# Shared expert's four up blocks moved from the combination into the routing stage and behind the third expert

## What is computed

```python
def swiglu(x, w1, w3, w2):
    return (jax.nn.silu(x @ w1) * (x @ w3)) @ w2

def moe_ffn(xs, router_w, router_bias, exp_w1, exp_w3, exp_w2, sh_w1, sh_w3, sh_w2):
    scores = jax.nn.sigmoid((xs @ router_w).astype(jnp.float32))
    ...                                   # idx, w: the 6 experts of a token and their weights
    yg = lax.map(expert_block, (xg, blk_e)).reshape(P, D) * slot_w[:, None]
    routed = jax.ops.segment_sum(yg, slot_tok, num_segments=T + 1)[:T]
    return routed + swiglu(xs, sh_w1, sh_w3, sh_w2)
```

## Time and profile before

| | us |
|---|---|
| median of 3 runs | 2116.54 (2116.13 to 2123.39) |
| the profiled execution's own time | 2121.22 |
| its span in the trace | 2119.4 |
| TensorE matmul busy | 1847.9 (87%) |
| TensorE weight load busy | 983.2 (46%) |
| VectorE busy | 864.2 (41%) |
| ScalarE busy | 458.9 (22%) |
| GpSimd busy | 389.3 (18%) |
| moved by DMA | 625.11 MB, mean 295 GB/s |

### The profile page before, as it was taken

One profiled execution on the slowest core, in us unless ns is written; L12 is line 12 of the kernel. 1 busy time (PEld: TensorE's weight loads), 2 busy tenths in 40 slices (PEclk: granted clock), 3 DMA queues, 4 the chain that ended last, 5 costly groups with the idle time before them and its releaser, 6 DMA issues.

```text
span 2119.4 us, 30756 instructions
## 1 busy us (share of the span) xinstructions
PE 1847.9 (87%) x9520; PEld 983.2 (46%) x9521; DVE 864.2 (41%) x1525; ACT 458.9 (22%) x823; POOL 389.3 (18%) x577
## 2 busy tenths in 40 slices
PE   5999999886998889887999998877888899988996
PEld 3455555434544444444444443344444444544543
DVE  1556767566322222222116499575222212222226
ACT  4144444221111011111011554330111111111112
POOL 0010000011111111111105388012111111111113
PEclk9999999997999999999999999898999999999998
DMA  9488011357999999999988102257999999999955
GB/s 402 182 335 339 1 40 48 151 218 269 397 410 402 398 394 393 404 399 394 373 357 307 76 1 119 86 243 280 391 405 403 399 395 406 390 406 392 395 185 209
DMA packets 95681, 625.11 MB, mean 295 GB/s; under 512 B 16128, under 2 KB 16256, under 8 KB 57472
## 3 DMA queue, kind: packets, MB, share of 16 engines
q1 hardware_dynamic: 44640, 499.70, 58.7%
q0 software_dynamic: 26112, 79.72, 10.4%
q10 hardware_dynamic: 24864, 44.84, 5.8%
HBM read 563.38 MB, written 76.28 MB: 302 GB/s over the span
## 4 chain that ended last, share of the span: by engine, by line
PE 56%; DMA 26%; DVE 8%; POOL 5%; issue 3%; ACT 2%; SPq 0%; POOLq 0%; ACTq 0%; DVEq 0%
DMA ring<-in 23%; PE PS L1171 10%; PE PS L1165 9%; PE PS L1178 5%; PE PS L1192 4%; PE PS L1203 4%; PE PS L1392 3%; POOL work L649 3%; PE PS L1129 3%; PE PS L1082 3%; PE PS L1053 2%; PE PS L1120 2%; PE PS L1015 2%; PE PS L1092 2%; POOL work L617 2%
## 5 line engine op out<-in xcount | busy, mean ns | idle before, releaser
L1171 PE MATMUL PS<-ring,work 128*64 128x256 f32 x3360 | 420.1, 406 | 112.9 <-DMA ring<-in 91.9
L1171 PEld LDWEIGHTS PS<-ring,work 128*64 128x64 f32 x3360 | 260.7, 146 | 248.4 <-DMA ring<-in 97.8
L1581 DVE TENSOR_TENSOR work<-work,PS 64x256 f32<-64x256 f32 x105 | 44.4, 423 | 524.9 <-ACT work L716 523.0
L1178 PE MATMUL PS<-ring,work 128*64 128x512 f32 x840 | 203.3, 605 | 1.3 <-DVE work L1593 1.2
L1165 PE MATMUL PS<-ring,work 128*128 128x512 f32 x400 | 184.1, 615 | 22.4 <-DMA ring<-in 16.1
L569 POOL COPY col_i<-idx 128x1 int32 (+1 forms) x128 | 23.4, 182 | 799.9 <-PE PS L1203 792.4
L1587 DVE COPY work<-PS 128x1024 f32<-128x1024 f32 x128 | 156.8, 1225 | 16.7 <-PE PS L1203 12.8
L575 POOL DMA_INDIRECT work<-h_rows,col_i x128 | 125.1, 978 | 166.0 <-issue 166.0
L1203 PE MATMUL PS<-cst,work 128*128 128x128 f32 x1040 | 142.4, 281 | 14.0 <-DMA work<-h_rows,col_i 14.0
L716 ACT ACTIVATE work<-PS 64x256 f32<-64x256 f32 x105 | 39.5, 376 | 517.9 <-PE PS L1171 515.6
L1203 PEld LDWEIGHTS PS<-cst,work 128*128 128x128 f32 x1040 | 115.0, 142 | 67.1 <-issue 52.4
(11 more groups left out here) (264 smaller groups left out, 2200.7 us busy)
## 6 DMA issues: line engine op xcount, KB each, us to landing
ring<-in SPq DMA_DIRECT2D x156, 2048.0 KB, 8.6
ring<-in SPq DMA_DIRECT2D x132, 1024.0 KB, 10.8
y_rows<-sq POOLq DMA_DIRECT2D x2, 14336.0 KB, 59.5
y_rows<-work ACTq DMA_DIRECT2D x210, 128.0 KB
ring<-in SPq DMA_DIRECT2D x3, 4096.0 KB, 15.4
y_rows<-work ACTq DMA_DIRECT2D x46, 256.0 KB
ring<-in SPq DMA_DIRECT2D x2, 3072.0 KB, 17.2
work<-in SPq DMA_DIRECT2D x2, 2048.0 KB, 17.0
```

The source lines that it names most:

```text
L1171: last = mm(bank(6)[64 * q:64 * q + 64, 0:F], lhs(c)[:, 0:64], w13(s)[:, q, c, :], start=(c == 0), stop=(c == DC - 1), tile_position=(0, 6 ...
L1178: last = mm(bank(4)[64 * q:64 * q + 64, :], actT[par][:, kk, 0:64], w2(s)[:, kk, q * 512:(q + 1) * 512], start=(kk == 0), stop=(kk == 1), ...
```

## The change

The four blocks and what feeds them move. Block (0,0) goes behind the transposes of the scores, a chunk each time ScalarE has written one of `hM` (in ScalarE's order, 6, 0, 7, 1, 2, 3, 4, 5). Of block (0,1) one chunk goes behind the first count matmul and one behind the next two, and six behind the last two; seven chunks of (1,0) follow, and the eighth goes behind the transposes of the first expert's rows. Block (1,1) goes behind unit 2 and waits for VectorE's table of result rows. They use PSUM banks 6, 5, 4 and 3. The silus and products move along. The up half of the shared weights is loaded into `work[:, 0:4096]`, where `acc` lies: in layer 0 with the router's weights once attention's matmuls are done, ahead of the last two units of the modulation's weights, and in layer 1 behind the convolution's layer norm, ahead of the last such unit. Since `acc` is taken, the rows are staged in the two gather buffers `xg` and the two result buffers `yb`, and ScalarE waits for their stores before it writes the first result there. The two clears of `xg` on GpSimd go; `prod_a` shares a tile with `prod_b`; the products of the shared expert get a tile of their own, `shared_sb`; and `dynamic_dma_scratch_size=8192` replaces the default of 16384. Two waits are added ahead of the shared down. Its core:

```diff
-        prod_a = work[:, TT * D:TT * D + NK * E].rearrange("p (k t e) -> p k t e", k=K, t=TT)
+        prod_a = prod_b = hT[:, DC * T + DC * E:DC * KEYS].rearrange("p (k t e) -> p k t e", k=K, t=TT)
+        staged = xg + yb
+        sh_up = work[:, 0:UP]
+        SHARED_BANK = (6, 5, 4, 3)
...
-                sp.wait_ge(m["up_ps"], E - 3)
-                sp.dma_start(slot_ap(SHARED)[:, 0:UP], sh_w[i][:, 0:UP]).then_inc(sh_in, 16)
...
-            for u in range(WO_UNITS, LATE):
+            for u in range(WO_UNITS, LATE - 2):
                 load_unit(u)
             sp.wait_ge(o_ps, NPAIR)
             load_router(0)
+            load_shared(0)
+            for u in range(LATE - 2, LATE):
+                load_unit(u)
...
-            for u in range(LATE, UNITS):
+            for u in range(LATE, UNITS - 1):
                 load_unit(u)
+            sp.wait_ge(nrm_out, 8 * J_LN + DC)
+            load_shared(1)
+            load_unit(UNITS - 1)
...
-                for n in range(2):
-                    nc.gpsimd.memset(xg[n], 0.0).then_inc(cleared, 1)
...
-                    A(acc[:, t, :], bank(1 if t % 2 == 0 else 4, 2), ACT.Copy).then_inc(hrow_sb, 1)
+                    A(staged[t], bank(1 if t % 2 == 0 else 4, 2), ACT.Copy).then_inc(hrow_sb, 1)
...
+                a.wait_ge(hd_out, 64 * (i + 1))
                 either(0, lambda big: store(0, 0, 0, big))
...
+                def shared_up(blk, a, chunks, wait=None):
+                    for c in chunks:
+                        if wait:
+                            wait(c)
+                        last = mm(bank(SHARED_BANK[2 * blk + a]), sh_w13[:, a, c, blk * 128:blk * 128 + 128], hM[:, c, :],
+                                  start=(c == SHARED_ORDER[blk, a][0]), stop=(c == SHARED_ORDER[blk, a][-1]))
+                        if c == SHARED_ORDER[blk, a][-1]:
+                            last.then_inc(sh_ps, 1)
...
-                pe.wait_ge(nrm_out, 8 * (J_FFN0, J_FFN1)[i] + DC)
+                pe.wait_ge(sh_in, 16 + 32 * i)
+                shared_up(0, 0, APPLY_ORDER, lambda c: pe.wait_ge(nrm_out, 8 * (J_FFN0, J_FFN1)[i] + APPLY_ORDER.index(c) + 1))
...
+                pe.wait_ge(hrow_sb, TT + i * TT)
+                shared_up(0, 1, range(0, 1))
...
+                shared_up(0, 1, range(1, 2))
...
+                shared_up(0, 1, range(2, DC))
+                shared_up(1, 0, range(0, DC - 1))
                 turn_rows(0, 16, 0)
+                shared_up(1, 0, range(DC - 1, DC))
...
                 unit(2, slot_of(2), slot_of(1), 32, 32, 0)
+                pe.wait_ge(rows_rdy, i + 1)
+                shared_up(1, 1, range(DC))
...
-                pe.wait_ge(sh_in, 32 * (i + 1))
-                shared_up(0, 0)
...
-                shared_up(0, 1)
-                pe.wait_ge(sh_gate, 1 + 2 * i)
-                shared_up(1, 0)
-                pe.wait_ge(sh_act, 1 + 2 * i)
-                shared_up(1, 1)
+                pe.wait_ge(sh_in, 32 * (i + 1))
                 pe.wait_ge(sh_act, 2 + 2 * i)
...
                 extra_rows()
+                shared_product(0)
                 rows_out(0, 0, 0)
...
                 act_out(2, 1, 0)
+                shared_product(1)
...
-                    if n == 10:
-                        shared_product(1)
...
-    nc = _bacc.Bacc("TRN2", target_bir_lowering=False, num_devices=1)
+    nc = _bacc.Bacc("TRN2", target_bir_lowering=False, num_devices=1, dynamic_dma_scratch_size=8192)
```

More of the change, by code:

```diff
@@ L202, in build @@
         select_to_cmpa = work[:, at_select:o[0]]
-        shared = [work[:, at_select - TT * E + n * T:at_select - TT * E + (n + 1) * T] for n in range(2)]
+        shared_sb = sb("shared_sb", [128, 2 * T])
+        shared = [shared_sb[:, n * T:(n + 1) * T] for n in range(2)]
         assert o[0] <= 12800
@@ L429, in load_router, with load_shared @@
                 sp.dma_start(bias_sb[:, :], router_bias[i].partition_broadcast(128)).then_inc(rw_in, 16)
+            def load_shared(i):
+                sp.dma_start(sh_up, sh_w[i][:, 0:UP]).then_inc(sh_in, 16)
             def load_moe(i):
@@ L749, in store, with shared_silu @@
                          .then_inc(y_out[par], 16)
+                def shared_silu(blk):
+                    a.wait_ge(sh_ps, 2 * blk + 1 + 5 * i)
+                    A(shared[blk], bank(SHARED_BANK[2 * blk]), ACT.Silu).then_inc(sh_gate, 1)
+                shared_silu(0)
                 a.wait_ge(big_rdy, i + 1)
+                shared_silu(1)
                 either(0, lambda big: silu(0, 0, 0, big))
                 either(1, lambda big: silu(1, 0, 1, big))
+                a.wait_ge(hd_out, 64 * (i + 1))
                 either(0, lambda big: store(0, 0, 0, big))
@@ L764, in moe @@
                 a.sem_inc(m["t_yev"], 1)
[L766 to L770, removed]
                 a.wait_ge(unit_rdy, i + 1)
@@ L1230, in rows_of @@
                     last.then_inc(hrow_ps, 1)
+                def shared_up(blk, a, chunks, wait=None):
[6 more added lines that the diff above has]
+                            last.then_inc(sh_ps, 1)
+                SHARED_ORDER = {(b, a): APPLY_ORDER if (b, a) == (0, 0) else range(DC) for b in range(2) for a in range(2)}
                 pe.wait_ge(scoreT_rdy, i + 1)
@@ L1290, in moe @@
                 unit(0, slot_of(0), None, 32, 16, 0)
+                pe.wait_ge(sh_gate, 2 + 3 * i)
                 unit(1, slot_of(1), slot_of(0), 32, 32, 1)
@@ L1307, in moe @@
                 either(E - 1, lambda big: down(E - 1, 1, slot_of(E - 1), big))
-                def shared_up(blk, a):
-                    for c in range(DC):
-                        last = mm(bank(3 * a), w13(SHARED)[:, a, c, blk * 128:blk * 128 + 128], hM[:, c, :], start=(c == 0), stop=(c == DC - 1))
-                    last.then_inc(sh_ps, 1)
-                pe.wait_ge(sh_in, 32 * (i + 1))
-                shared_up(0, 0)
                 many = nc.tensor.value_load(unit_i[0:1, XMAX:XMAX + 1], min_val=0, max_val=XMAX)
@@ L1711, in weights, with shared_product @@
                                                 wsum.unsqueeze(1).to_broadcast([128, K, TT]), ALU.mult, ALU.mult))
+                def shared_product(blk):
+                    dve.wait_ge(sh_ps, 2 * blk + 2 + 5 * i)
+                    dve.wait_ge(sh_gate, blk + 1 + 3 * i)
+                    V.tensor_tensor(shared[blk], shared[blk], bank(SHARED_BANK[2 * blk + 1]), ALU.mult).then_inc(sh_act, 1)
                 dve.wait_ge(count_ps, 3 + 3 * i)
```

18 lines of the change are left out of this document (9 added, 9 removed).

## The result

The changed kernel takes 2125.75 us (median of 20 runs, 2121.58 to 2133.73) and the kernel before, over its own 20 runs, 2120.71 (2113.03 to 2125.58). The ratio is 1.0028 with a 95% interval of 1.0019 to 1.0037: slower by 5.9 us (4.0 to 7.8), and so within the half per cent called no change. Forecast were 2125.0 us and +8.5 us. The forecast difference lies a little above that interval. That the time itself came out 0.75 us from the forecast is partly luck: the kernel before came out 4.2 us above the three runs known at the time.

What follows compares the result with a forecast made beforehand. Each expert loop was taken to end when its weights have come through DMA (busy share 1.01); 8.6 + 9.0 - 7.4 - 1.7 = +8.5 us on the median 2116.54 gave 2125.0 us, range 2109 to 2134.

Steps and rivals of the forecast that it cites:

- term 1: Start of each expert loop: fifteen chunks ahead of the first expert delay its up and the first refill request, +8.6 us.
- term 3: End of each loop: without block (0,0) the extra unit's up starts earlier, then waits for its weights, -7.4 us.
- Term 2: Behind the third expert: block (1,1) delays refill requests, paid less what the DMA queue had in store, +9.0 us.
- the 2.2 + 1.8 + 1.0 of the prediction: Behind the third expert: queue's store in layers 0 and 1, and layer 1's idle time filled ahead of unit 3's up.
- Term 4: The combination: blocks leave TensorE, shortening VectorE's wait in layer 0, and the second product leaves VectorE's chain, -1.7 us.
- (a): Expert loops: the loop absorbs both delays at its start, about 2107.5 us or 2104; chance 0.16.
- (b): Routing stage: TensorE's clock falls within block (0,0), delaying the row transposes, some 5 us a layer, 2135 us; chance 0.14.

Runs made afterwards that it cites:

- the one with slots exchanged: Changed kernel with the ring slots of the extra unit and of the shared down weights exchanged; ratio 0.9995 to the kernel before.
- the first two kernels: The kernel before, and that kernel with only the scratch for GpSimd's descriptors halved (8192 for 16384), ratio 0.999.

## Why the prediction was right, and where it was off

**The direction and the whole were right:** a small loss, +5.9 us against a forecast of +8.5, from two delays at the loops' start, less a gain at their end. By the table, the loops end 6.6 us a layer later than before (627.3, the mean of the changed kernel and the one with slots exchanged, against 620.6, the mean of the first two kernels), 13.2 together; the extra unit gives 2.7 a layer back (the ten layers of the changed kernel, of (1,1) twice and of the three kernels with blocks in mid-loop and slots not exchanged have a mean of 19.3, against 22.05), 5.4 together; what is left to 5.9 is -1.9. That the sum came within 2.6 us of the measured difference is in part luck: term 1 was too high and the gain of term 3 too large, and the two errors go against each other.

**Term 2, block (1,1), +9.0:** right in place, mechanism and, nearly, in size. Moved away alone it gave 10.8 us by the ratio and 2 x 4.9 by the loops' ends; doubled, it cost its full length. The queue's store of 2.2 and 1.8 us was read from the earlier trace rows, and the changed kernel's DMA view shows it used up. TensorE's timelines show where it was used. Take the end of a unit's up, counted from the end of its layer's first up, against the mean of the first two kernels (which differ by up to 3.2 us in this). In layer 0 of the changed kernel unit 3 is 6.9 us late, unit 8 3.6, unit 30 4.2 and the last 3.9; with (1,1) twice the same units are 13.7, 10.3, 9.3 and 9.4 us late. Some 3.3 us are made good once, within five units, and the rest stays. In layer 1 of the changed kernel it is 6.3, 4.7, 4.9 and 7.1. With three blocks in mid-loop, unit 27 of layer 0, behind the second of them, is 4.0 us late and unit 30 only 0.2.

**Term 1, the fifteen chunks, +8.6: mis-sized.** The first up ended 1.1 and 4.8 us later against its layer's scores, 5.9 together; averaged over the kernels that keep the chunks up to there (changed, slots exchanged, doubled, (1,1) moved) and against the mean of the first two, 1.1 and 3.6, so 4.7. The step that failed is the start of the sum. It put the first count matmul where it was; that came 1.4 and 1.7 us earlier. Counted from there, the first up did end 2.6 and 6.4 us later, as forecast. Most of the 1.4 and 1.7 is that the two clears on GpSimd, taken at nothing, had slowed VectorE's one-hot matrices by a us: put back, they bring the count matmul to +24.4, of +24.6 and +24.9 before. The 2.5 us that the sum adds behind the count matmuls, and the 3.0 of its high end, were the author's estimate for chunks at the lower clock, set between what two other groups had lost after idle time, 2.0 us of 5.68 and 3.0 of 17.00; no run shows either for the chunks. In their place the changed kernel's trace showed 2.3 us in layer 0, with a granted clock of 0.50 from 490 to 495 us and 0.85 in the next 5, and in layer 1 2.07 + 2.07 + 12.58 - 13.1 = 3.6, with 0.50 from 1430 to 1435 us and 0.65 in the next 5. The first up did keep full clock behind the chunks: 3.67 us in both layers, at a granted clock of 1.00. What reached the first up goes on to the loop's end where the block doesn't follow: with the block in mid-loop the loops end 1.8 us a layer later than before (622.4 against 620.6). In the whole time the chunks' price stays open between 5.7 us (fourteen left out) and nothing (fifteen gone, two blocks in mid-loop). By the first-up column the two delays bring 4.7 + 14.0 us to a pair of loops that ended 13.2 later: 5.5 us were swallowed once, near the 2.2 + 1.8 + 1.0 of the prediction, and the lateness of the units puts that behind the block, as the prediction did.

**Term 3, the loops' end, -7.4:** the right wait, named in advance, at 5.4 on average; in the changed kernel's own trace it is 3.7 in layer 0 and 0.4 in layer 1. The extra's weights came 10.2 us after their issue in layer 0 and 13.5 in layer 1, against 11.2 and 10.4 before, and the wait and the slower up after it were as forecast. (By the earlier trace rows the up was to start 5.4 and 5.6 us earlier, not 5.3 and 5.5, which would have made the term -7.6.) That the weights were what was late next is shown by the exchange of slots, which took 7.0 us off.

**Term 4, the combination, -1.7:** about -1.9 by what is left over, which is a remainder and no measurement. In the two traces the stretch from the end of the extra unit's down to the end of VectorE's residual went from 52.6 to 50.0 us in layer 0 and from 54.1 to 51.0 in layer 1, and what follows the last residual from 15.6 to 17.0; but the kernel before with half the scratch has 52.0 and 51.9 for that stretch, so the size isn't settled. VectorE's wait for the last transposes came to 0.89 us in both layers, where 0.8 had been forecast for layer 0 and no change for layer 1. TensorE's last 16 transposes did run at a lower clock in both layers, 3.78 and 3.79 us at a granted clock of 0.50; in layer 1 of the kernel before they took 2.05 us at 1.00.

**The rivals.** (a) falls: delays ahead of requests weren't absorbed, as the doubled block shows. Its premise holds elsewhere, though: in the middle of the loop three blocks of 7 us a layer left no gap in the part of the stream that was read, and their lateness was gone a few units later. At the loop's start it did not hold. (b) falls: the granted clock was 1.00 from 470 to 478 us, through block (0,0), and the row transposes took 1.91 us and started 1.0 us later than before.

## What to carry to other kernels

In a kernel like this one, work of an idle engine is cheap inside a stretch that waits for transfers only where the transfers' queue has more in store than the work takes; the test is the requests' size less the bytes moved up to the moment of the delay. Where the ring had just filled, that store was some 2 us, and a delay of 7.0 us was paid at 4 to 5; with the store used up, the next 7.0 us were paid whole; twenty units later the same work left no gap and little lateness. And when a block ahead of a wait goes, ask at once which transfer ends last next: here a slot that was free one unit earlier gave 7.0 us, more than the move had lost.

## What the runs showed of the hardware that was not expected

VectorE's bf16 operations here were slowed by clears on GpSimd that shared no data with them: 24 of 128x128 took 5.03 us beside 2.03 us of clears, 4.00 without them, and 5.15 with them put back on another tile. That is 1.0 to 1.15 us lost to some 2 us of clears; by what way the clears reach VectorE's operations, no run here shows.
